# A hybrid decoder block with 32 experts on one core: a flat expert loop on TensorE and six matmul widths instead of five

## The reference, cut to what matters

```python
logits = xt @ router_w + router_b
top_val, top_idx = lax.top_k(logits, TOP_K)          # 4 of 32 experts for each of 1024 rows
gates = jax.nn.softmax(top_val, axis=-1)
...
gu = xb @ w_gu[e] + b_gu[e]                          # (n, 1024) @ (1024, 2048)
glu = jnp.minimum(gu[:, :D_FF], SWIGLU_LIMIT)
lin = jnp.clip(gu[:, D_FF:], -SWIGLU_LIMIT, SWIGLU_LIMIT)
act = glu * jax.nn.sigmoid(SWIGLU_ALPHA * glu) * (lin + 1)
return act @ w_down[e] + b_down[e]                   # (n, 1024) @ (1024, 1024)
```

## Time and profile before

| | us |
|---|---|
| median of 3 runs | 2460.75 (2460.61 to 2462.6) |
| the profiled execution | 2460.42 |
| its span, first to last instruction | 2458.7 |
| TensorE matmuls busy | 2332.1 (95% of the span) |
| VectorE busy | 764.3 (31%) |
| ScalarE busy | 609.6 (25%) |
| GpSimd busy | 250.5 (10%) |
| mean granted clock of TensorE | 0.974 of full speed |

### The profile page before, as it was taken

The page is one execution under the profiler, slowest core; times in us unless marked ns, Lnnn a source line. Parts: engine busy times, 40 slices in busy tenths (PEclk is TensorE's granted clock), DMA queues, the critical chain, the costliest instruction groups (busy, mean ns, idle before and its releaser), DMA issues.

```text
span 2458.7 us, 41234 instructions
## 1 busy us (share of the span) xinstructions
PE 2332.1 (95%) x15394; PEld 1994.0 (81%) x15395; DVE 764.3 (31%) x1819; ACT 609.6 (25%) x1284; POOL 250.5 (10%) x227
## 2 busy tenths in 40 slices
PE   7999999899969999989999999999999999999994
PEld 3343545456649999989999999999999999999994
DVE  2161321477752232222323222321222222222222
ACT  2112111244402222222222222211221222222223
POOL 1000000021130111001011101100100000010011
PEclk8999999899979999999999999999999999999997
DMA  7000000211146899869889889975976788798686
GB/s 283 35 0 0 1 0 35 101 52 53 44 141 219 271 293 287 278 214 276 280 277 298 265 261 293 296 220 183 290 241 207 215 266 251 240 286 276 208 255 217
DMA packets 440328, 485.95 MB, mean 198 GB/s; under 512 B 23965, under 2 KB 417357, under 8 KB 440252
## 3 DMA queue, kind: packets, MB, share of 16 engines
q1 hardware_dynamic: 419996, 450.33, 56.1%
q0 software_dynamic: 20080, 34.88, 6.7%
q10 hardware_dynamic: 208, 0.16, 0.0%
HBM read 473.41 MB, written 49.58 MB: 213 GB/s over the span
## 4 chain that ended last, share of the span: by engine, by line
PE 93%; issue 2%; DVE 2%; DMA 1%; ACT 1%; POOL 0%; SPq 0%; ACTq 0%; POOLq 0%; DVEq 0%
PE PS L923 64%; PE PS L599 14%; PE PS L783 5%; PE PS L884 2%; PE PS L866 2%; PE PS L723 1%; PE PS L756 1%; PE PS L745 1%; PE PS L675 1%; PE PS L678 0%; PE PS L802 0%; DVE unit L1400 0%; PE PS L631 0%; DMA out_dram<-unit 0%; PE PS L574 0%
## 5 line engine op out<-in xcount | busy, mean ns | idle before, releaser
L923 PE MATMUL PS<-pairA,unit 128*128 x12288 | 1588.1, 291 | 25.9 <-issue 23.3
L923 PEld LDWEIGHTS PS<-pairA,unit 128*128 128x128 f32 x12288 | 1561.7, 191 | 45.0 <-issue 34.5
L599 PE MATMUL PS<-pairA,unit 128*128 128x512 f32 (+1 forms) x544 | 245.4, 609 | 2.5 <-issue 2.5
L1646 DVE TENSOR_SCALAR unit<-PS,cur_b 128x256 f32<-128x256 f32 x256 | 112.1, 479 | 368.4 <-PE PS L923 353.5
L1178 ACT ACTIVATE unit<-PS,cur_b 128x256 f32<-128x256 f32 x256 | 107.5, 471 | 457.0 <-PE PS L923 457.0
L599 PEld LDWEIGHTS PS<-pairA,unit 128*128 128x128 f32 (+1 forms) x544 | 101.9, 191 | 138.2 <-issue 137.6
L1165 ACT ACTIVATE unit<-unit 128x512 f32<-128x512 f32 x128 | 80.6, 630 | 482.1 <-DVE unit L1646 470.0
L1169 ACT ACTIVATE unit<-PS,cur_b 128x256 f32<-128x256 f32 x256 | 107.5, 471 | 321.4 <-PE PS L923 321.4
L517 POOL DMA_INDIRECT unit<-h_dram,cur_x x66 | 69.5, 1053 | 1011.1 <-DVE cur_x L1640 994.6
L1653 DVE TENSOR_SCALAR unit<-unit 128x512 f32<-128x512 f32 x128 | 54.7, 427 | 344.8 <-ACT unit L1169 344.8
L536 POOL DMA_INDIRECT acc_dram<-pairA,cur_y x66 | 105.9, 1604 | 531.7 <-ACT pairA L1149 521.0
(11 more groups left out here) (228 smaller groups left out, 1245.2 us busy)
## 6 DMA issues: line engine op xcount, KB each, us to landing
unit<-in_expert_w_gu_dram SPq DMA_DIRECT2D x256, 1024.0 KB, 5.3
unit<-in_expert_w_down_dram SPq DMA_DIRECT2D x128, 1024.0 KB, 6.7
unit<-in_w_in_dram SPq DMA_DIRECT2D x6, 2048.0 KB, 14.5
pairB<-in_x_dram SPq DMA_DIRECT2D x16, 512.0 KB, 9.9
unit<-in_w_out_dram SPq DMA_DIRECT2D x2, 2048.0 KB, 12.0
h_dram<-pairA SPq DMA_DIRECT2D x8, 512.0 KB
acc_dram<-pairB SPq DMA_DIRECT2D x8, 512.0 KB
pairB<-acc_dram SPq DMA_DIRECT2D x8, 512.0 KB, 6.4
```

Of the source, the lines that this page charges most:

```text
L599: ins = pe.matmul(ps, lhs, rhs, start=(k == 0), stop=(k == KD - 1))
L923: ins = pe.matmul(bank(s)[:, ITEM * j:ITEM * j + w], slot_w[s][:, k, P * j:P * j + P], xa_cols[:, ITEM * k:ITEM * k + KD * ITEM + w][:, ba ...
L1646: ins = dve.tensor_scalar(glu_t[:, c % 2, ITEM * j:ITEM * j + ITEM], bank(gate_slot)[:, ITEM * j:ITEM * j + ITEM], cur_b[:, 2 * c + j:2 * ...
```

## The change

TensorE's loop becomes one flat loop of 96 passes (3 times 32), with the place in an item kept in a register `phase` and all per-item registers set at the end of phase 2. It doesn't look at the item count. The passes of extra items follow in a second copy of the pass, of width 256 only, behind one comparison. `landed` and `drained` become one register `moved`; for that, `bank_read` counts in steps of 16 on ScalarE, VectorE and in every wait. WIDTHS has six entries, and the comparisons test the first width alone, then halve the rest.

```diff
-WIDTHS = [128, 144, 168, 192, ITEM]
+WIDTHS = [132, 144, 156, 168, 184, ITEM]
...
-                mid = len(widths) // 2
-                with pe.If(n <= widths[mid - 1]):
-                    by_width(n, widths[:mid], body)
+                near = 1 if widths[0] == WIDTHS[0] else len(widths) // 2
+                with pe.If(n <= widths[near - 1]):
+                    by_width(n, widths[:near], body)
                 with pe.Else():
-                    by_width(n, widths[mid:], body)
+                    by_width(n, widths[near:], body)
...
-            with pe.Fori(0, ITEMS // GROUP + 1) as g:
-                with pe.If(GROUP * g < last):
-                    with pe.Fori(0, GROUP):
-                        i = pe.snap(item, min_val=0, max_val=ITEMS - 1)
-                        with pe.If(i < last):
-                            n = pe.snap(n_next, min_val=0, max_val=SEQ)
-                            n_done = pe.snap(n_last, min_val=0, max_val=SEQ)
-                            pe.reg_mov(n_last, n)
-                            with pe.Fori(0, 3) as p:
-                                block0 = pe.snap(half, min_val=0, max_val=KD * ITEM)
...
+            def one_pass(widths):
+                n = pe.snap(n_now, min_val=0, max_val=SEQ)
+                block0 = pe.snap(half, min_val=0, max_val=KD * ITEM)
...
+                by_width(n, widths, four_slabs)
+                p = pe.snap(phase, min_val=0, max_val=2)
+                with pe.If(p < 1):
+                    n_done = pe.snap(n_last, min_val=0, max_val=SEQ)
...
+                    i = pe.snap(item, min_val=0, max_val=ITEMS - 1)
+                    pe.load(n_next, item_n[0:1, bass.ds(i + 1, 1)])
+                    pe.reg_mov(phase, 1)
+                with pe.Else():
+                    with pe.If(p < 2):
...
+                        pe.reg_mov(phase, 2)
+                    with pe.Else():
+                        pe.reg_add(first_six, first_six, 5)
+                        pe.reg_mov(half, 0)
+                        pe.reg_mov(phase, 0)
+                        pe.reg_mov(n_last, n_now)
+                        pe.reg_mov(n_now, n_next)
+                        pe.reg_add(item, item, 1)
+                    pe.reg_add(all_eight, all_eight, 4)
+                pe.reg_add(moved, moved, 16)
+
+            with pe.Fori(0, 3 * N_EXP):
+                one_pass(WIDTHS)
+            with pe.If(last > N_EXP):
+                with pe.Fori(N_EXP, ITEMS) as extra:
+                    with pe.If(extra < last):
+                        with pe.Fori(0, 3):
+                            one_pass([ITEM])
             pe.wait_ge(rhs_ready, 8 * last + 4)
             for s in range(SLOTS):
-                pe.wait_ge(bank_read[s], 3 * last + 1)
+                pe.wait_ge(bank_read[s], 48 * last + 16)
...
-                                ins.then_inc(bank_read[up_slot], 1)
+                                ins.then_inc(bank_read[up_slot], 16)
```

More of the change, by code:

```diff
@@ L894, in _ @@
             last = pe.value_load(n_items[0:1, 0:1], min_val=N_EXP, max_val=ITEMS)
-            n_last, n_next, landed, drained, first_six, all_eight, half = (pe.alloc_register(n) for n in (
-                "n_last", "n_next", "landed", "drained", "first_six", "all_eight", "half"))
-            pe.load(n_next, item_n[0:1, 0:1])
+            n_last, n_now, n_next, phase, moved, first_six, all_eight, half, item = (pe.alloc_register(n) for n in (
+                "n_last", "n_now", "n_next", "phase", "moved", "first_six", "all_eight", "half", "pe_item"))
@@ L898, in _ @@
+            pe.load(n_now, item_n[0:1, 0:1])
             pe.reg_mov(n_last, SEQ)
-            for reg, value in ((landed, 16), (drained, 1), (first_six, 4), (all_eight, 4), (half, 0)):
+            for reg, value in ((moved, 16), (first_six, 4), (all_eight, 4), (half, 0), (phase, 0), (item, 0), (n_next, 0)):
                 pe.reg_mov(reg, value)
-            item = pe.alloc_register("pe_item")
-            pe.reg_mov(item, 0)
-            with pe.Fori(0, ITEMS // GROUP + 1) as g:
-                with pe.If(GROUP * g < last):
-                    with pe.Fori(0, GROUP):
-                        i = pe.snap(item, min_val=0, max_val=ITEMS - 1)
-                        with pe.If(i < last):
-                            n = pe.snap(n_next, min_val=0, max_val=SEQ)
-                            n_done = pe.snap(n_last, min_val=0, max_val=SEQ)
-                            pe.reg_mov(n_last, n)
-                            with pe.Fori(0, 3) as p:
-                                block0 = pe.snap(half, min_val=0, max_val=KD * ITEM)
[L914 to L952, removed]
@@ new lines, in one_pass, with four_slabs @@
+            def one_pass(widths):
+                n = pe.snap(n_now, min_val=0, max_val=SEQ)
+                block0 = pe.snap(half, min_val=0, max_val=KD * ITEM)
+                def four_slabs(w):
+                    pe.wait_ge(rhs_ready, first_six)
+                    for s in range(SLOTS):
+                        pe.wait_ge(slot_in[s], moved)
+                        pe.wait_ge(bank_read[s], moved)
+                        for j in range(2):
+                            for k in range(KD):
+                                if s == 0 and j == 0 and k == 6:
+                                    pe.wait_ge(rhs_ready, all_eight)
+                                ins = pe.matmul(bank(s)[:, ITEM * j:ITEM * j + w],
+                                                slot_w[s][:, k, P * j:P * j + P],
+                                                xa_cols[:, ITEM * k:ITEM * k + KD * ITEM + w][:, bass.ds(block0, w)],
+                                                start=(k == 0), stop=(k == KD - 1))
+                        ins.then_inc(slab_done[s], 1)
+                by_width(n, widths, four_slabs)
+                p = pe.snap(phase, min_val=0, max_val=2)
+                with pe.If(p < 1):
+                    n_done = pe.snap(n_last, min_val=0, max_val=SEQ)
+                    with pe.If(n_done <= P):
+                        turn_y(1)
+                    with pe.Else():
+                        turn_y()
+                    i = pe.snap(item, min_val=0, max_val=ITEMS - 1)
[3 more added lines that the diff above has]
+                    with pe.If(p < 2):
+                        i = pe.snap(item, min_val=0, max_val=ITEMS - 1)
+                        n_after = pe.snap(n_next, min_val=0, max_val=SEQ)
+                        pe.wait_ge(y_evac, 4 * i + 4)
+                        with pe.If(n_after <= P):
+                            turn_rows(i + 1, 1)
+                        with pe.Else():
+                            turn_rows(i + 1)
+                        pe.reg_add(first_six, first_six, 3)
+                        pe.reg_mov(half, KD * ITEM)
+                        pe.reg_mov(phase, 2)
+                    with pe.Else():
+                        pe.reg_add(first_six, first_six, 5)
[6 more added lines that the diff above has]
+                pe.reg_add(moved, moved, 16)
@@ L1141, in _ @@
             for s in range(SLOTS):
-                act.sem_inc(bank_read[s], 1)
+                act.sem_inc(bank_read[s], 16)
             def take_y(i):
@@ L1163, in _ @@
                                 gate_slot, up_slot = 2 * (c % 2), 2 * (c % 2) + 1
-                                act.wait_ge(bank_read[gate_slot], 3 * i + c // 2 + 2)
+                                act.wait_ge(bank_read[gate_slot], 48 * i + 16 * (c // 2) + 32)
                                 act.activation(glu_s[:, c % 2, :], glu_t[:, c % 2, :], ACT.Sigmoid,
@@ L1179, in _ @@
                                                          bias=cur_b[:, 2 * NF + 2 * s + j:2 * NF + 2 * s + j + 1])
-                                ins.then_inc(bank_read[s], 1)
+                                ins.then_inc(bank_read[s], 16)
                             act.reg_add(item, item, 1)
@@ L1636, in _ @@
                             nxt = dve.value_load(item_col[0:1, bass.ds(i + 1, 1)], min_val=0, max_val=N_EXP * LISTS - 2)
-                            dve.wait_ge(bank_read[SLOTS - 1], 3 * i + 1)
+                            dve.wait_ge(bank_read[SLOTS - 1], 48 * i + 16)
                             dve.tensor_copy(cur_b[:, :], b_all[:, bass.ds(e, 1), :]).then_inc(cur_b_ready, 1)
@@ L1648, in _ @@
                                                             cur_b[:, 2 * c + j:2 * c + j + 1], LIMIT, ALU.add, ALU.min)
-                                ins.then_inc(bank_read[gate_slot], 1)
+                                ins.then_inc(bank_read[gate_slot], 16)
                                 dve.wait_ge(sig_ready, 4 * i + c + 1)
                                 step.do(dve.tensor_tensor(glu_s[:, c % 2, :], glu_t[:, c % 2, :], glu_s[:, c % 2, :], ALU.mult))
-                                dve.wait_ge(bank_read[up_slot], 3 * i + c // 2 + 2)
+                                dve.wait_ge(bank_read[up_slot], 48 * i + 16 * (c // 2) + 32)
```

## The result

The changed kernel takes 2841.23 us (2838.06 to 2846.38, 4 runs) against 2460.68 us before, a ratio of 1.155 (1.153 to 1.157): 15% slower. The forecast was 2940 us, the range 2425 to 3200.

What follows compares the result with a forecast made beforehand. TensorE, busy 95% of the span, was taken as the bound. From 2460.4 us, widths (-17.5) and control (-10) gave -27, instruction fetches +509 (374 + 135): 2942, rounded 2940 us; range 2425 to 3200.

Steps and rivals of the forecast that it cites:

- The sign and its cause: TensorE's loop: a sixth body overflows eight held instruction blocks, so code is refetched; slower, chance 0.61, fetch cost +509 us.
- This repeats in all 96 passes: TensorE's loop end: asking for a ninth block evicts the loop's start, so every pass waits; +374 us.
- The price of a pass: TensorE's branch back to missing code: mean 3.9 us lost per pass, plus second waits for 10 items, +135 us.
- The clock: TensorE after long stops: a lowered clock lengthens the next pass, up to 2.5 us each, +240 us, upper bound only.
- the straight line: TensorE pass length by width: 0.107 us per column from 144 to 256, extended down to give 14.40 us at 132.
- Held in two groups of four: TensorE's instruction store: a fetch outside both groups of four blocks replaces the group not in use.
- The widths: TensorE's matmul passes: finer widths save 23.1 us, 132 instead of 128 costs 5.6; net -17.5 us, between -23 and -5.
- the chord: TensorE pass length interpolated between 128 and 144 columns: 132 costs 0.35 us over 128, +17.8 us in all.
- The control: TensorE's gaps between passes: the flat loop has less branching at an item's end; -10 us, between 0 and -15.
- The code fits after all: Rival, TensorE's instruction store: the loop and block ahead fit, no refetching; 2433 us, 2425 to 2445; chance 0.34.
- Milder loss: only items with wide bodies: Rival, TensorE's loop: only 15 items meet missing code, three passes each at 3.5 us; about 2590 us; chance 0.06.
- Weights that come too late: Rival, weight DMA in narrow stretches: would take at most some us off the gain; counted within the 0.34 rival.

Runs made afterwards that it cites:

- experiment 2: The old nest of loops with the six new widths and new order of comparisons, against the kernel before: 2865.82 us, ratio 1.1645.
- experiment 5: The changed kernel with 176 TensorE instructions added ahead of the loop, against the kernel before: 2438.92 us, ratio 0.990.
- experiment 7: The changed kernel with 220 TensorE instructions added ahead of the loop, against the kernel before: 2849.21 us, ratio 1.157.
- experiment 4: The changed kernel with 128 TensorE instructions added ahead of the loop, against the kernel before: 2476.82 us, ratio 1.005.
- experiment 6: The changed kernel with 88 TensorE instructions added ahead of the loop, against the kernel before: 2697.21 us, ratio 1.095.
- experiment 1: The flat loop with the five old widths and old halving of comparisons, against the kernel before: 2447.81 us, ratio 0.994.

## Why the prediction was right, and where it was not

**The sign and its cause: right.** The forecast said that a sixth body makes the loop end inside an eighth block, that the block ahead is then a ninth, and that something needed is pushed out. The compiled loop has 1741 instructions (1745 forecast) and ends some 34 to 48 instructions into that block, if the boundaries lie where the ring rule puts them, inside the forecast's 15 to 80. Experiments 2, 5 and 7 show the cause: the loss comes with the sixth width, goes when the loop lies in seven blocks, and is back when it lies in eight. The Trainium skill's page "Runtime: NRT & Kernel Launch", section on instruction fetch mechanics, gives TensorE 2048 instructions in blocks of 256; eight places are what the fetch counts fit. The same section says that a taken branch waits for a DMA when its target lies outside "the current 2-page window". That such a branch waits agrees, with up to 3.4 to 6.4 us in the rows above; a window of two pages does not, as the kernel before, whose loop lies in seven blocks, ran from 1060 to 2420 us without one fetch, so the measurement decides against it. "Advanced Engine Details and Errata" of the Trainium skill, section ISA Cache, gives 128 KB on TensorE and lines of 16 KB, which is eight, but then "Only 2 cache lines!"; the eight agree with the fetch counts, the two do not.

**"This repeats in all 96 passes": the step that failed.** It took for granted that b5 is held, too, so that b8 must push out something in use. But b5 holds only the end of the 184 body and the start of the 256 one. As long as items are narrow, eight blocks are held, by the ring rule b0 to b4 and b6 to b8; not one fetch was seen in 540 us. Passes of 256 or 184 run through b5, passes of 168 enter b4 and so call for b5; that is the ninth block. The 21 passes of these seven experts pay, the other 75 hardly (17 us in all).

**The price of a pass: far too small, and so the sum came out near.** The forecast had one wait of 4.9 us, two for some items. Of these 21 passes 14 have nine fetches, and a full gap holds four or five waits in a row. The reason, read from the code and the ring rule, is where the comparisons stand: `by_width` puts each at the start of a body, so on its way to the sixth body the sequencer steps through b0, b1, b3 and b4, and each step waits for a block. After the pass at 1842 us five branches in a row took 1.9, 6.4, 3.3, 4.7 and 3.1 us. Set against the version of experiment 5, pass by pass, the 21 passes have 341 us more gap and 43 us more between their first and last matmul, together 18.3 us each; all other passes together have 17 us more. That makes 401 us, the difference of the two spans (2838.1 - 2437.1). The forecast had 509 us for all 96 passes, 5.3 each: a count 4.6 times too high by a price 3.5 times too low. The total missed by only 99 us of 2940 because the two errors met; that it came so near was luck.

**The clock** was a bound only, and it is in the 43 us: the granted clock was 0.79 from 1842 to 1884.4 us, and 0.50 (the lower level of 1.2 GHz) in 1870 to 1890.5 us, in and after the time in which TensorE stood idle; it was 1.00 in the same kind of stretch of experiment 5. A pass of 184 columns took 23.24 us in the chain above, where the straight line gives 19.95.

**"Held in two groups of four"**: refuted by experiments 4 and 6. It stood on one event before, and the ring gives the same event.

**The widths: right in size.** -17.5 us were forecast. From experiment 1 to experiment 5 the span falls by 10.2 us, and the latter has 5.4 us of new stop before item 18 (the first visit to b5) and 1.1 us of later start; that leaves 16.7. The bodies were right one by one: 14.57 us for 132 columns against 14.46 for 128, first to last matmul, so 0.11 more, as the straight line said, not the 0.35 of the chord.

**The control: right.** -10 forecast, 0 to -15 as bounds; 12.9 us by the medians of experiment 1 against the kernel before as first measured, 14.6 against the runs beside it.

**The rivals.** "The code fits after all" is what experiment 5 built on purpose, with 2438.9 us against the 2433 worked out for it. "Milder loss: only items with wide bodies" had the right kind of items and a chance of 0.06; its 15 items at 3.5 us a pass were too many and too cheap. Weights that come too late were seen nowhere: TensorE was busy for 538.72 of 540 us at a DMA share of 0.92.

**What the profile was to show.** Fetches on q8 were to be 200 to 300, and are 204; but not through the whole expert part. The closing branch was to take 3 to 9 us, and takes up to 6.4. "Issue" of hundreds of us ahead of the matmul is there. The passes of 132 and 156 columns have the lengths forecast within 0.2 us.

**What stays open.** The ring's rules were fitted on three kernels and then forecast the fetches of three more (11 seen for 10, 117 for 115, 184 for 198). They give 7 to 15% too many fetches where the loss is full, so some detail is missing, perhaps when two requests fall together. Another rule with the same counts is not excluded.

## What to carry to other kernels

Count the instructions of a runtime loop on TensorE as you would count SBUF: in the blocks that it touches plus the one ahead, and look at the fetch queue's row and at the longest branch, not at the median. If those were more than eight, the loop here ran well on narrow items and lost 18 us a pass on wide ones, and 20 instructions more ahead of it (156 to 176) turned 2809 us into 2439; so leave a block free, or put the comparisons together ahead of the bodies, which wasn't tried here. The finer widths were worth 17 us and the flat control 13, and either survives only if the code fits.

## What the runs showed of the hardware that was not expected

- The place of a loop decides: 156, 176 and 220 added instructions ahead of it gave 2809, 2439 and 2849 us with the same loop.
- The state depends on the path taken: the same loop ran 540 us without a fetch, and then lost some 18 us in each wide pass, beginning with the item of 217 rows; by the ring rule because that item called for one more block.
- A branch that waited for code took 1.9 to 7.5 us of the sequencer in these runs. A single such wait behind pass 0 cost TensorE 1.6 to 2.4 us less than it lasted (5.34 and 4.87 us of wait, 3.49 and 2.49 us of idle time in the kernel before); in a row they added up: the five at 1864 to 1884 us, 19.4 us together, left TensorE idle for 18.7 us.
